# Value and gate projection of all eight token tiles first, its weights kept on chip, and most weight blocks cast from DRAM to DRAM

## What is computed

```python
p = x @ w_in                              # columns B_a C_a v_a val_b gate_b g_a g_b, 1024 each
y_a = (b_a * conv3(c_a * v_a)) @ w_out_a
u = val_b * sigmoid(gate_b)
u = conv31(u, conv_b_w) + conv_b_bias
y_b = silu(layernorm(u, ln_b_gamma, ln_b_beta)) @ w_out_b
mix = (sigmoid(g_a) * y_a + sigmoid(g_b) * y_b) @ w_o
x1 = layernorm(alpha * x + mix)
x2 = layernorm(alpha * x1 + relu(x1 @ w_up)**2 @ w_down)   # 4096 hidden channels
```

## Time and profile before

| | us |
|---|---|
| before, three runs | 2332.71, 2338.74, 2348.6 (median 2338.74) |
| the profiled execution | 2336.12 |
| its span, first to last instruction, slowest core | 2334.6 |
| spans of the eight cores | 2304.1 to 2334.6 |
| mean granted TensorE clock of the cores | 0.969 to 0.974 of full speed |

### The profile page before, as it was taken

One profiled execution on the slowest core, in us unless ns is written; L12 is line 12 of the kernel. 1 busy time (PEld: TensorE's weight loads), 2 busy tenths in 40 slices (PEclk: granted clock), 3 DMA queues, 4 the chain that ended last, 5 costly groups with the idle time before them and its releaser, 6 DMA issues.

```text
span 2334.6 us, 33063 instructions; the slowest of 8 cores (2304.1 to 2334.6 us)
## 1 busy us (share of the span) xinstructions
PE 2162.4 (93%) x11351; PEld 964.0 (41%) x11568; DVE 872.5 (37%) x1247; ACT 896.5 (38%) x1416; POOL 579.2 (25%) x528
## 2 busy tenths in 40 slices
PE   4888899997999989999899998999999999999996
PEld 1343344433444434444344443444444444444442
DVE  2253552234612246123632237222470325523604
ACT  0222354222552225522364224633256323542462
POOL 1022222331323313132303214032130422221221
PEclk9898999998999999999999999999999999999998
DMA  9799697797887997878666675447644486434462
GB/s 169 165 217 181 182 153 126 171 205 209 168 169 201 236 252 173 203 218 243 182 186 181 201 203 186 144 154 220 215 146 153 133 243 189 164 141 166 145 195 76
DMA packets 109971, 423.75 MB, mean 182 GB/s; under 512 B 14064, under 2 KB 55280, under 8 KB 68080
## 3 DMA queue, kind: packets, MB, share of 16 engines
q1 hardware_dynamic: 82656, 291.53, 39.4%
q0 software_dynamic: 19088, 115.42, 27.7%
q10 hardware_dynamic: 8064, 14.68, 1.7%
HBM read 457.24 MB, written 62.98 MB: 223 GB/s over the span
## 4 chain that ended last, share of the span: by engine, by line
PE 73%; DMA 15%; DVE 6%; issue 3%; ACT 1%; SPq 1%; POOL 1%; DVEq 0%; ACTq 0%; POOLq 0%
PE ps L269 69%; DMA wsl<-wblk 4%; PE ps L433 4%; DMA xft<-xblk 3%; DMA u0d<-u0h 2%; DMA wbf<-wsl 2%; DVE sgt L292 2%; DMA u0d<-u 1%; DVE res L292 1%; SPq L109 1%; DMA rep<-u0d 1%; DVE sbf L279 1%; DMA yblk<-tt 1%; DVE cvb L279 0%; DVE sgt L284 0%
## 5 line engine op out<-in xcount | busy, mean ns | idle before, releaser
L269 PE MATMUL ps<-xbf,wsl 128*128 128x512 bf16 x3564 | 835.0, 388 | 53.4 <-DMA wsl<-wblk 29.1
L269 PE MATMUL ps<-bx,wsl 128*128 128x512 bf16 x2496 | 564.9, 380 | 10.0 <-ACT bx L275 5.9
L269 PEld LDWEIGHTS ps<-xbf,wsl 128*128 128x128 bf16 x3648 | 356.9, 99 | 499.2 <-issue 103.5
L269 PE MATMUL ps<-h,wsl 128*128 128x512 bf16 x2442 | 542.7, 380 | 17.4 <-DMA wsl<-wblk 14.5
L275 ACT ACTIVATE tA<-ps 128x512 f32<-128x512 f32 x448 | 266.0, 595 | 493.4 <-PE ps L269 468.2
L269 PEld LDWEIGHTS ps<-bx,wsl 128*128 128x128 bf16 x2560 | 249.0, 98 | 313.6 <-issue 17.9
L269 PEld LDWEIGHTS ps<-h,wsl 128*128 128x128 bf16 x2496 | 244.6, 98 | 311.4 <-issue 19.4
L279 POOL TENSOR_TENSOR tt<-tt,rstd 128x512 f32<-128x512 f32 x178 | 243.6, 1368 | 97.8 <-ACT rstd L275 74.3
L279 POOL TENSOR_TENSOR tt<-res,mu 128x512 f32<-128x512 f32 x112 | 150.8, 1346 | 449.0 <-ACT mu L275 245.5
L275 ACT ACTIVATE sq<-res 128x512 f32<-128x512 f32 x112 | 70.3, 630 | 409.4 <-DVE res L292 409.2
L279 DVE TENSOR_TENSOR tA<-ps,tA 128x512 f32<-128x512 f32 x128 | 88.2, 691 | 312.3 <-PE ps L269 306.9
(11 more groups left out here) (55 smaller groups left out, 994.6 us busy)
## 6 DMA issues: line engine op xcount, KB each, us to landing
wsl<-wbf SPq DMA_DIRECT2D x198, 1024.0 KB, 6.0
wsl<-wblk POOLq DMA_DIRECT2D x85, 1024.0 KB, 13.4
wbf<-wsl SPq DMA_DIRECT2D x36, 1024.0 KB, 12.8
rep<-u0d SPq DMA_DIRECT2D x256, 135.0 KB, 4.8
xft<-xblk POOLq DMA_DIRECT2D x64, 256.0 KB, 9.5
yblk<-tt ACTq DMA_DIRECT2D x56, 256.0 KB, 8.1
u0d<-u SPq DMA_DIRECT2D x64, 128.0 KB, 6.1
xbf<-xblk POOLq DMA_DIRECT2D x7, 1024.0 KB, 13.2
```

Source lines behind the costliest of these rows:

```text
L269: last = e.matmul(bank_ap, lhsT=l, rhs=r, start=(start and idx == 0), stop=(stop and idx == n - 1))
```

## The change

- `stage_F` runs for all eight tiles at the start, in the order 2, 3, 4, 5, 6, 7, 0, 1. The four B blocks are cast once, straight into the buffer `h` (32 KB on each partition, which holds up's result later on), and stay there. The gate's product goes into `apre` instead of the three buffers `u0`, and is stored from there to `u0d`. The first six convolutions of tile 0 stand in F of tiles 0 and 1.
- The tiles of x are loaded for F, and those of 2 to 7 again in their passes: six more loads of 1 MB (written) on POOL.
- `convert` is a new DMA on POOL that casts a block from `wblk` to its copy in `wbf`, DRAM to DRAM. 24 blocks get it: six of A and eight of S3 during F, two of w_o in S1A of tile 0, w_up 0 to 3 in pass 0, w_down 0 to 3 in pass 1. The other eight (w_up 4 to 7, w_down 4 to 7) are still cast on their way into a slot and stored from there; w_down 0 to 3 is cast once into a slot as well. Rows of `wbf` are now 64 elements further apart.
- `stD.finish(1)` moves from down's end to behind the first piece of the next S3, and all eight pieces of the second norm into S3.
- `xload` is issued by ACT instead of POOL.
- In mix, the six running sums of squares (sumQ) go from DVE to POOL.
- `rep` has three buffers instead of two, and the first spreads of tile i+1 are issued by the convolutions of tile i. `ident4`, `hsm` and `u0h` now lie in parts of `xft` and `cvb`.

The diff, cut to its core:

```diff
-NREP = 2
+NREP = 3
-    wbf = nc.dram_tensor("wbf", [NBLK, 128, 4096], BF16).ap()
+    wbf = nc.dram_tensor("wbf", [NBLK, 128, 4096 + WPAD], BF16).ap()[:, :, 0:4096]
...
-        seq = [B0 + k for k in range(4)] + [A0 + k for k in range(6)]
+        seq = [A0 + k for k in range(6)]
         for i in range(NPASS):
-            if 0 < i < NPASS - 1:
-                seq += [B0 + k for k in range(4)]
             seq += [S30 + k for k in range(8)] + [WO0, WO0 + 1]
...
+        BG = {b: 0 for b in range(S30, UP0 + 4)}
+        BG.update({DN0 + k: 1 for k in range(4)})
+        STORE = {UP0 + k: 0 for k in range(4, 8)}
+        STORE.update({DN0 + k: 1 for k in range(4, 8)})
+
+        def convert(*blks):
+            for blk in blks:
+                S.dma("pool", castsem[blk], wbf[blk], wblk[blk], writes=[("wbf", blk)])

         def w_load(L):
             blk, s = seq[L], L % NS
-            if occ[L] <= store_at(blk):
+            if occ[L] < BG[blk] if blk in BG else occ[L] <= STORE[blk]:
                 S.dma("pool", wcsem[s], wsl[s][:], wblk[blk], writes=[("wsl", s)])
...
+        def wB(j, kc, which):
+            o = kc * 512 + ((j % 2) * 2 + which) * 128
+            return hB[j // 2][:, o:o + 128]
...
-                    add(sumQ[k][:], sumQ[k][:], sqv, reads=[("sumQ", k), sqid], writes=[("sumQ", k)])
+                    tten(eng, sumQ[k][:], sumQ[k][:], sqv, ALU.add, reads=[("sumQ", k), sqid],
+                         writes=[("sumQ", k)])
...
         def xload(i, e_):
-            S.dma("pool", xfsem[e_ % 4], xft[e_ % 4][:], xblk[i, :, e_, :], reads=[],
-                  writes=[("xft", e_ % 4)])
+            S.dma("act", xfsem[e_ % 4], xft[e_ % 4][:], xblk[i, :, e_, :], reads=[],
+                  writes=[("xft", e_ % 4)] + (["ident4", ("hsm", 0), ("hsm", 1)] if i == 0 else []))
...
-        stage_F_start()
+        convert(A0)
+        for k in range(8):
+            def f0_each(j, k=k):
+                if k == 6:
+                    if j in (1, 2, 3):
+                        spread(0, j - 1)
+                    if j in (5, 7):
+                        conv(0, (j - 5) // 2, stC)
+                elif k == 7:
+                    if j % 2 == 1:
+                        conv(0, 2 + j // 2, stC)
+            stage_F(k, f0_each)
+            if k + 2 < 8:
+                x_load(FO[k + 2])
+                convert(*list(range(A0, UP0))[2 * k + 1:2 * k + 3] if k < 2 else ())
+                if k == 2:
+                    convert(A0 + 5, S30)
+                elif k > 2:
+                    convert(S30 + 2 * (k - 3) + 1, S30 + 2 * (k - 3) + 2)
...
-                if not last:
-                    take(ln2_tasks, 1)
+                if not last and i > 0:
+                    if j == 0:
+                        stD.finish(1)
+                    else:
+                        take(ln2_tasks, 2 if j == 1 else 1)
```

More of the change, by code:

```diff
@@ L29 @@
 NS = 4
-NU = 3
+WPAD = 64
 NMAIN = 8
@@ L172, in build_nc @@
         ps = [st.enter_context(nc.psum_tensor(f"ps{i}", [128, T], F32)) for i in range(8)]
+        ident4 = xft[0][:, 0:32]
+        hsm = [xft[1][:, HL * i:HL * i + HL] for i in range(2)]
+        u0h = [cvb[1][:, HL * i:HL * i + HL] for i in range(2)]
         cwb = sq[1][:, 0:8 * 4 * KS].rearrange("p (j k) -> p j k", k=4 * KS)
@@ L312, in F_mm @@
-        def F_mm(i, j, s, bv, bgk):
-            q0 = (j % 2) * 2
+            S.dma("sp", udsem[i % 2][j], u0d[j, :, HL + i * T:HL + (i + 1) * T], apre[:, j, :],
+                  reads=[("apre", j)], writes=[("u0d", i % 2, j)])
+        def F_mm(i, j, bv, bgk):
             for which, b in ((0, bv), (1, bgk)):
-                mm(ps[b][:, :], [(wk(s, kc, q0 + which), xbf[i % 2][:, kc, :]) for kc in range(8)],
-                   reads=[("wsl", s), ("xbf", i % 2)], writes=[("ps", b)])
-        def F_halo(j, s):
-            q0 = (j % 2) * 2
+                mm(ps[b][:, :], [(wB(j, kc, which), xbf[i % 2][:, kc, :]) for kc in range(8)],
+                   reads=hk(j // 2) + [("xbf", i % 2)], writes=[("ps", b)])
@@ L320, in F_halo @@
+        def F_halo(j):
             hv, hg = nb(), nb()
             for which, b in ((0, hv), (1, hg)):
-                mm(ps[b][:, 0:HL], [(wk(s, kc, q0 + which), xhbf[:, kc, :]) for kc in range(8)],
-                   reads=[("wsl", s), "xhbf"], writes=[("ps", b)])
-            rh = rt("hsm", 4)
-            act(hsm[rh][:], ps[hg][:, 0:HL], AF.Tanh, reads=[("ps", hg)], writes=[("hsm", rh)], scale=0.5)
+                mm(ps[b][:, 0:HL], [(wB(j, kc, which), xhbf[:, kc, :]) for kc in range(8)],
+                   reads=hk(j // 2) + ["xhbf"], writes=[("ps", b)])
+            rh = rt("hsm", 2)
+            act(hsm[rh], ps[hg][:, 0:HL], AF.Tanh, reads=[("ps", hg)], writes=[("hsm", rh)], scale=0.5)
@@ new lines, in stage_F @@
+        def stage_F(k, each=None):
+            i = FO[k]
+            js = range(8)
+            if k == 0:
+                js = range(2, 8)
+                bks = [(nb(), nb()) for _ in range(2)]
+                for j in range(2):
+                    for which, b in enumerate(bks[j]):
+                        mm(ps[b][:, :], [(wB(j, kc, which), xbf[i % 2][:, kc, :]) for kc in range(4)],
+                           reads=["w0a", "x0a"], writes=[("ps", b)], start=True, stop=False)
+                for j in range(2):
+                    for which, b in enumerate(bks[j]):
+                        mm(ps[b][:, :], [(wB(j, kc, which), xbf[i % 2][:, kc, :]) for kc in range(4, 8)],
+                           reads=hk(0) + [("xbf", i % 2)], writes=[("ps", b)], start=False, stop=True)
+                    F_gate(i, j, *bks[j])
+            for j in js:
@@ L379, in spread @@
+                if i == 0:
+                    F_halo(j)
+                if each is not None:
+                    each(j)
         def spread(i, j):
-            r = j % NREP
+            r = (8 * i + j) % NREP
             src = u0d[j].rearrange("(g c) n -> c g n", c=32)
@@ L750, in build_nc @@
             if i + 2 < NPASS:
-                S.dma("pool", xbsem[i % 2], xbf[i % 2][:], xblk[i + 2], writes=[("xbf", i % 2)])
+                x_load(i + 2)
             stM = stC if last else stD
@@ L800, in build_nc @@
                     down_part(range(8), RES, stD, d_each)
-                    stD.finish(1)
                     ln2_tasks = [(lambda e_=e_, i=i: ln2_apply(i, RES, e_)) for e_ in range(8)]
```

131 lines of the change are left out of this document (48 added, 83 removed).

## The result

The changed kernel takes 2370.64 us (median of ten executions), the kernel before 2338.36 us (ten, alternating with it on the same chip). The ratio is 1.0102 with a 95% interval of 1.0077 to 1.0128: the change makes the kernel 1% slower, where 2219 us and a gain of 5% were forecast. Some executions of every kernel fall in a slower state of the chip and are left out of a ratio (those kept took 2357.8 to 2376.16 us for the changed kernel), so it is not always the quotient of the medians. The profiled execution took 2376.16 us (span 2374.6, slowest core 7; the eight cores 2337.7 to 2374.6).

The account below looks back on a forecast made before the run. PE, busy 2162 of 2335 us, was the bound; only its waits and slow clock could be won. 314.5 (head) + 245.7 + 243.7 + 4 x 240.7 + 429.4 + 19 = 2215 us span, 2219 us forecast, range 2192 to 2262.

Parts of the forecast that it names:

- the cover of the casts: F stages: 29.1 us of DMA against 27.6, arrears 9 us in six, covered because x is issued ahead of the casts.
- The head: Program start through F of all tiles and S1A: ends at 314.5 us including 6 of waits, a gain of 30 us.
- Four `xload` on ACT ahead of S3 cost nothing: Start of S3 in each pass: no cost, since PE has eight banks to run ahead in.
- The norm of mix: End of mix: fifth `xft` late by 1 to 3 us instead of 8.5; 3 us a pass left for wait and clock.
- rival 3: Mix stays late: ACT's `xft` lands no sooner and POOL's sums add their lock; +24 us, 2243; chance 0.12.
- The second norm in S3: Eight pieces, 16 POOL operations, at most 27 us, must be through within S3's 61 us; they are.
- no waits for casting loads: Weight slots: PE's 43.6 us of waits for casting loads go; from pass 2 on nothing is cast but x.
- the cast's price in engine time: DRAM-to-DRAM casts: 6.4 + 3.3 = 9.7 us of DMA engine time each.
- no waits of PE at down's end: Down's norm: `stD.finish` gets 32 matmuls (6.9 us) in front of it, so that wait is gone.
- the sums on POOL as a draw: Mix: DVE and POOL alternating take 1.95 us a piece against 2.07 on DVE before, nearly a draw.
- Rival 4: Slower than before: casts at their upper bound, c = 26.2 us, deciding from c = 21; +187, 2406 us; chance 0.03.
- Passes 6 and 7: Last two passes: only mix improves, 14.7 to 12 us above the floor, gain 2.7; 429.4 us, tail of 19 stays.

Follow-up runs that it names:

- after: The changed kernel itself, as measured against the kernel before: 2370.64 us, ratio 1.0102.
- e1: Changed kernel with A and S3 blocks cast on their way into a slot and stored from there, not DRAM to DRAM during F; ratio 1.0129 to the kernel before.
- e2: Changed kernel with each row of `wbf` written in four padded pieces of 2 KB, the same bytes; ratio 0.9998 to the kernel before.
- e12: Changed kernel with e5's repairs, u of tiles 2 to 7 stored two tiles at once, and last S3 and w_o casts held later by dependencies; ratio 0.9713, 2268.73 us.
- e3: Changed kernel where in pass 0 only the first `xload` claims `ident4` and only the second `hsm`; ratio 1.0033 to the kernel before.
- e4: Changed kernel with the 1 MB load of x issued behind mix instead of ahead of it; ratio 0.9884 to the kernel before.
- e6: The kernel before with only the 1 MB load of x moved from ahead of mix to behind it; ratio 0.9906 to the kernel before.
- e11: e10 with the first two w_down casts also moved from S3 of pass 1 to its S1A; ratio 0.9801 to the kernel before.
- e5: Changed kernel with the changes of e3 and e4 together; ratio 0.9808 to the kernel before.
- e9: e5 with mix's sums of squares back on DVE and the load of x waiting for mix's seventh product; ratio 0.9839 to the kernel before.
- e10: Changed kernel with e5's repairs, two-tile u stores, and last three S3 and two w_o casts placed in S1A of tile 0; no ratio, profiled 2286.84 us.

## Why the prediction was wrong

**The step that failed is the cover of the casts.** I costed F's DMA as a sum of engine time: two casts, a load of x and "1 MB of stores to `u0d`" at 3.3 us by their bytes, 29.1 us against a stage of 27.6, and asked only whether x would be late. The sum of engine time was right: in 60 to 90 us q0 wrote 3.54 MB in 0.942 x 30 us, 8.0 us a MB, where I had (6.4 + 19.4) / 3 = 8.6, and PE never waited for x in after. But in these traces a transfer in another queue waits its turn packet by packet. While q0 has work, a 1 KB packet of a store waits for a packet of 8 KB, about 0.93 us (0.942 x 30 x 16 / 486, the mean over all of q0's packets). A 128 KB store has eight for each of 16 engines, so an estimate is 7.4 us at best, and 60 us for the eight stores of a stage, in 27.6. (When q0 runs dry, as at 110 to 120 us, the stores catch up.) The stores fell behind, `apre` ran out of free pieces, and tile 0's halo and first spread came behind the backlog. It cost what is in the table's first row: 33.55 us at the halo and 12.1 at `apre`, of +47.3.

e1 shows that the casts are the cause, e2 that turns are taken by packets and not by bytes, and that smaller packets of the casts take away the waits at `apre`, and e12 that the hole closes when the casts come later. The Trainium skill (DMA: Bandwidth & Descriptors, on queues, rings and completion order) states that each DMA engine goes round the queues with work at the granularity of packets. The trace agrees, by the 432 and 430 packets in the hole of after and by e2's 1210 and 1203. That rule spoke against this change, and I had not weighed it. The same passage of the Trainium skill puts about 9 to 17 descriptors into a typical packet; how many a row takes no run shows, but here a turn was a single row: of the 296 rows of 1 KB that start in the hole (220 to 250 us), 249 are followed 55 or 56 ns later by the start of a packet of q0. (The records do not name the engine; at 112 to 118 us, with no cast under way, none is.)

**The head** otherwise held. With the stores mended it ended at 315.4 to 320.9 us in the six cores of e12 without the slower clock (324.2 in core 7), against 320.9.

**"Four `xload` on ACT ahead of S3 cost nothing"** was wrong in pass 0 alone. The buffers share their space with `ident4` and `hsm`, and through these names each load waited for the one before: 31.28 us on ACT, 13.88 on PE. The diff shows the line; I read it as one wait, not as a chain. e3 shows it.

**The norm of mix** is rival 3, whose mechanism I had given 0.12. `xft` lands no sooner in ACT's queue, as it said. But I had read the earlier trace rows as a matter of POOL's queue, "the 1 MB load that delayed it is in another queue", and that was the argument against. e4 and e6 show that the load does the delaying from any queue. In passes 2 to 5 of after the four waits are 6.92, 8.27, 6.81 and 11.90 us, 33.9 where I left 3 each. Behind such waits comes the clock, for which I had forecast above 0.98 (0.954 to 0.968 over the span of the cores): 0.97 to 0.98 in these passes of after, 0.99 to 1.00 in core 3 of e12.

**The second norm in S3** was too simple in pass 1: the second norm's eight pieces "must be through within S3", and by my count they were. I had counted POOL's operations and not the stores of y that free their buffers. Beside a cast of w_down these land in 20.0 us (the median of five in 680 to 740 us of after), and POOL stands:

```profile
712.05 1.26 POOL L278 TENSOR_TENSOR tt<-res,mu 128x512 f32<-128x512 f32 x1 [22.93 <-DMA yblk<-tt]
...
721.34 0.35 ACTq L101 DMA_DIRECT2D xft<-xblk  x1
...
731.30 0.69 DVE L291 SCALAR_TENSOR_TENSOR res<-xft,ps 128x512 f32<-128x512 f32 x1 [22.54 <-DMA xft<-xblk]
```

ACT waits for POOL's piece, its `xft` loads stand behind that, and DVE's fifth product of mix comes 22.54 us late; PE waits 17.46 us at 739.11. e12 still has this (POOL 22.12, PE 12.78). That its first cause is the w_down casts is supported by e11, where the wait fell to 3.40 us, but e11 has the casts late enough to make a new one. The rest of the 23 us of passes 0 and 1 I did not take apart.

**Right** were: no waits for casting loads (2.2 us), F at 27.6 us a stage where nothing stops it, the cast's price in engine time, no waits of PE at down's end, the sums on POOL as a draw (e5 and e9). Rival 4 came out on the side of the result, but by another mechanism: it asked for a cast of 21 us of engine time, and there is none.

**Passes 6 and 7** lost 28.2 us in the profiled execution: a wait of 1.72 us at mix, one of 5.79 for `bx`, and the clock. PE is busy 445.48 us for 2117 matmuls there and 419.71 us for the same 2117 in core 3 of e12. From 2230 to 2357 us core 7's granted clock is 0.81 (last section), which costs about 0.19 x 127 = 24 us; no run ties that to the change.

## What to carry to other kernels

Before putting a large transfer beside small ones, count the packets and not the bytes: where a queue with large packets was never empty here, another queue got one packet through for each of them (432 and 430 in 30 us), so small-row stores need wider rows, or a time when the large transfer is not there. A transfer that is moved to another engine's queue is not out of the way of the one that delayed it. And the place of a DMA in the program means nothing on an engine that has nothing to wait for there (two of e10's casts went out over 90 us ahead of their stage): hold it by a dependency, in the kernel and in the experiment alike.
